# Weight slabs split in two halves and a straight-line GpSimd program in a two-layer retention, Fourier and convolution backbone

## What is computed

```python
for l in range(2):
    sh1, sc1, g1, sh2, sc2, g2 = split(silu(c) @ w_mod[l] + b_mod[l], 6)   # the same for ctx
    p = (rmsnorm(x) * (1 + sc1) + sh1) @ w_in[l]          # q, k, v, gate, fourier, conv columns
    y = concat([retention(q, k, v) * silu(gate),          # both directions, chunks of 128
                real(fft2(p_fourier)),                    # tokens x channels of a group
                p_b * dwconv3(p_c * p_h)])
    x = x + g1 * (y @ w_out[l])
    h = rmsnorm(x) * (1 + sc2) + sh2
    u = dwconv3(h @ w_up[l], w_conv[l]);  val, gate = split(u, 2)
    x = x + g2 * ((val * silu(gate)) @ w_down[l])
return rmsnorm(x, final_norm_g)
```

## Time and profile before

| | |
|---|---|
| time, median of 3 runs | 1671.29 us (1668.88 to 1674.12) |
| the profiled execution | 1678.89 us, its span 1677.0 us |
| mean granted TensorE clock | 0.976 |
| PE busy | 1600.7 us, 95%, 8780 matmuls |
| DVE busy | 955.4 us, 57% |
| POOL busy | 808.8 us, 48%, 636 instructions |
| slab loads | 210 of 512 KB, 3.3 us each from issue to landing |

### The profile page before, as it was taken

The page is one execution under the profiler, slowest core; times in us unless marked ns, Lnnn a source line. Parts: engine busy times, 40 slices in busy tenths (PEclk is TensorE's granted clock), DMA queues, the critical chain, the costliest instruction groups (busy, mean ns, idle before and its releaser), DMA issues.

```text
span 1677.0 us, 24126 instructions
## 1 busy us (share of the span) xinstructions
PE 1600.7 (95%) x8780; PEld 1332.2 (79%) x8780; DVE 955.4 (57%) x1310; ACT 326.3 (19%) x489; POOL 808.8 (48%) x636
## 2 busy tenths in 40 slices
PE   8989999999989999999999999999989999999997
PEld 2878788778777888888888887877767787887876
DVE  2797554378777775874288648454456441341445
ACT  2502111221312200220022214111222220220220
POOL 1244322465334454444444443443464676666663
PEclk9899999989899999999999999999999999999998
DMA  8344111243133343332333222231122222232222
GB/s 348 119 148 150 45 51 39 85 151 113 63 116 115 118 152 113 113 137 69 107 125 113 88 98 79 83 94 51 63 88 76 89 98 88 100 100 95 93 94 94
DMA packets 49635, 174.46 MB, mean 104 GB/s; under 512 B 6448, under 2 KB 6832, under 8 KB 48560
## 3 DMA queue, kind: packets, MB, share of 16 engines
q1 hardware_dynamic: 45504, 167.79, 29.5%
q10 hardware_dynamic: 4080, 5.94, 1.4%
HBM read 167.41 MB, written 2.10 MB: 101 GB/s over the span
## 4 chain that ended last, share of the span: by engine, by line
PE 48%; DVE 18%; issue 14%; POOL 9%; DMA 8%; ACT 2%; DVEq 1%; ACTq 0%; SPq 0%; POOLq 0%
PE pair L1005 40%; DMA raw<-in_slabs 7%; POOL w_lo L384 5%; DVE aux L616 4%; POOL w_hi L382 3%; DVE tg L947 2%; DVE tv L947 2%; PE pair L1054 2%; DVE hid_lo L975 2%; DVE tv L972 1%; PE aux L1213 1%; DVE modv L619 1%; DVE nt L705 1%; ACT tv L586 1%; ACT hid_hi L594 1%
## 5 line engine op out<-in xcount | busy, mean ns | idle before, releaser
L1005 PE MATMUL pair<-h_hi,w_hi 128*128 128x512 f32 x1888 | 573.9, 362 | 23.1 <-POOL w_lo L384 10.9
L1005 PE MATMUL pair<-h_lo,w_hi 128*128 128x512 f32 x1888 | 566.4, 358 | 5.6 <-DVE h_lo L721 3.8
L1005 PE MATMUL pair<-h_hi,w_lo 128*128 128x512 f32 x1888 | 562.8, 356 | 0.0
L384 POOL TENSOR_TENSOR w_lo<-raw,w_hi 128x1024 fp32r<-128x1024 f32 x210 | 536.7, 2556 | 17.5
L380 POOL TENSOR_TENSOR gate<-ones 128x1 f32<-128x1 f32 x210 | 56.4, 269 | 831.3 <-PE pair L1005 736.1
L1005 PEld LDWEIGHTS pair<-h_hi,w_hi 128*128 128x128 f32 x1888 | 312.7, 191 | 81.3 <-issue 18.8
L1005 PEld LDWEIGHTS pair<-h_lo,w_hi 128*128 128x128 f32 x1888 | 311.3, 190 | 64.6 <-DVE h_lo L721 12.3
L1005 PEld LDWEIGHTS pair<-h_hi,w_lo 128*128 128x128 f32 x1888 | 312.4, 191 | 50.6
L616 DVE CUSTOM_DVE_ANT_0 aux<-mod_slot,c_b 128x1024 f32<-128x1024 f32 x160 | 235.0, 1469 | 6.1 <-DMA mod_slot<-in_mods 3.3
L382 POOL TENSOR_SCALAR w_hi<-raw 128x1024 fp32r<-128x1024 f32 x210 | 224.0, 1067 | 0.1
L911 DVE SCALAR_TENSOR_TENSOR x<-pair,modv,x 128x256 f32 (+3 forms) x96 | 60.6, 658 | 187.7 <-PE pair L1005 187.7
(11 more groups left out here) (137 smaller groups left out, 1073.7 us busy)
## 6 DMA issues: line engine op xcount, KB each, us to landing
raw<-in_slabs SPq DMA_DIRECT2D x210, 512.0 KB, 3.3
mod_slot<-in_mods SPq DMA_DIRECT2D x80, 512.0 KB, 3.3
start_slot<-in_start_mods SPq DMA_DIRECT2D x8, 1024.0 KB, 13.5
x<-in_x SPq DMA_DIRECT2D x4, 768.0 KB, 18.1
rot<-kT ACTq DMA_DIRECT2D x32, 64.0 KB, 2.0
rot<-Y ACTq DMA_DIRECT2D x32, 64.0 KB, 2.1
out<-fin SPq DMA_DIRECT2D x8, 256.0 KB, 2.2
c_b<-in_c SPq DMA_DIRECT2D x1, 512.0 KB, 3.9
```

What stands on the lines that cost most here:

```text
L384: nc.gpsimd.tensor_tensor(w_lo[p][:, :], raw[p][:, :], w_hi[p][:, :].bitcast(fp32), ALU.subtract).then_inc(split, 1)
L1005: ins = nc.tensor.matmul(out[:, a:b], wt, xt[:, a:b], start=first and k == 0, stop=last and k == 2)
```

## The change

Each slab is split in two halves of four tiles. The first half of slab s waits for the landing and for a new count, `half_done[p]`, which TensorE raises after tile 3 of slab s - 2; the second half waits for `done` of slab s - 2. (Behind a context table, whose columns all lie in the first half, the first half waits for `done`.) The second half of a down slab with 7 blocks has 384 columns. TensorE begins a slab when its first half is split and waits for the second ahead of tile 4. `split` now counts four per slab; SyncE's waits are scaled and mean the same. The `gate` product is gone, and GpSimd's program is written out for all 210 slabs with constant waits. In the table products the halves t run outside, the blocks b inside, with a wait for the second half between. The output projection's tiles are stored in the order in which they are used.

```diff
+            def split_half(s, half):
+                p, n = s % 2, s // 2
+                a, b = (0, 4 * P) if half == 0 else (4 * P, slab_blocks(s) * P)
+                if half == 0:
+                    pool.wait_ge(loaded[p], 16 * (n + 1))
+                if n and half == 0 and not narrow(s - 2):
+                    pool.wait_ge(half_done[p], n)
+                elif n:
+                    pool.wait_ge(done, s - 1)
+                nc.gpsimd.tensor_scalar(w_hi[p][:, a:b], raw[p][:, a:b], 1.0, 1.0, ALU.mult, ALU.mult).then_inc(split, 1)
+                pool.wait_ge(split, 4 * s + 2 * half + 1)
+                nc.gpsimd.tensor_tensor(w_lo[p][:, a:b], raw[p][:, a:b], w_hi[p][:, a:b].bitcast(fp32),
                                         ALU.subtract).then_inc(split, 1)
+            for s in range(PLAN["end"]):
+                for half in range(2):
+                    split_half(s, half)
...
-                pe.wait_ge(split, 2 * s + 2)
+                pe.wait_ge(split, 4 * s + 2)
...
+                if n == 4:
+                    pe.wait_ge(split, 4 * s + 4)
...
+                if n == 3:
+                    ins.then_inc(half_done[p], 1)
...
-                    for b in range(FB):
-                        for t in range(2):
+                    for t in range(2):
+                        if t and n < NLC:
+                            pe.wait_ge(split, 4 * sl + 4)
+                        for b in range(FB):
...
+                        if t == 0:
+                            ins.then_inc(half_done[p], 1)
...
-        slabs.append(tiles(np.asarray(w_out)[l], KB))
+        slabs.append(tiles(np.asarray(w_out)[l].reshape(KB, P, D)[Y_ORDER].reshape(D, D), KB))
```

More of the change, by code:

```diff
@@ L63, with slab_blocks, narrow @@
 PLAN = stream_plan()
+def slab_blocks(s):
+    for l in range(DEPTH):
+        for g, n in enumerate(GROUPS):
+            if PLAN[l, "down", g] <= s < PLAN[l, "down", g] + KB:
+                return n
+    return KB
+def narrow(s):
+    return PLAN[0, "dft"] + NLC <= s < PLAN[0, "dft"] + NLC + NCC
 def pair_uses(s):
@@ L153, in build_program @@
     ones = new("ones", [P, 1])
-    gate = new("gate", [P, 1])
     root_probe = new("root_probe", [P, 1])
@@ L238, in build_program @@
     done = sem("slab_done")
+    half_done = [sem(f"half_slab_done{i}") for i in range(2)]
     drained = [sem(f"pair_drained{i}") for i in range(2)]
@@ L287, in load_slabs @@
                     for p in range(2):
-                        sp.wait_ge(split, 2 * (first + p - 1) + 4 * i)
+                        sp.wait_ge(split, 4 * (first + p - 1) + 8 * i)
                         load_slab(first + p + 2 * i, p)
@@ L335, in _ @@
                     for p in range(2):
-                        sp.wait_ge(split, 2 * (s + 1 + p) + 4 * i)
+                        sp.wait_ge(split, 4 * (s + 1 + p) + 8 * i)
                         load_slab(s + 2 + p + 2 * i, p)
@@ L372, in _ @@
             pool.wait_ge(fills, 2)
-            def split_slab(p, n, first):
-                pool.wait_ge(loaded[p], 16 * (n + 1))
-                if not first:
-                    pool.wait_ge(done, 2 * n + (p - 1))
-                nc.gpsimd.tensor_tensor(gate[:, 0:1], ones[:, 0:1], ones[:, 0:1], ALU.mult).then_inc(gate_done, 1)
-                pool.wait_ge(gate_done, 1)
-                nc.gpsimd.tensor_scalar(w_hi[p][:, :], raw[p][:, :], 1.0, 1.0, ALU.mult, ALU.mult).then_inc(split, 1)
-                pool.wait_ge(split, 4 * n + (2 * p + 1))
-                nc.gpsimd.tensor_tensor(w_lo[p][:, :], raw[p][:, :], w_hi[p][:, :].bitcast(fp32),
-                                        ALU.subtract).then_inc(split, 1)
-            for p in range(2):
-                split_slab(p, 0, True)
-            with pool.Fori(1, PLAN["end"] // 2) as i:
-                for p in range(2):
-                    split_slab(p, i, False)
+            def split_half(s, half):
[10 more added lines that the diff above has]
+                nc.gpsimd.tensor_tensor(w_lo[p][:, a:b], raw[p][:, a:b], w_hi[p][:, a:b].bitcast(fp32),
+                                        ALU.subtract).then_inc(split, 1)
+            for s in range(PLAN["end"]):
+                for half in range(2):
+                    split_half(s, half)
         @block.scalar
@@ L1008, in begin, with tile @@
             def begin(p, s, uses):
-                pe.wait_ge(split, 2 * s + 2)
+                pe.wait_ge(split, 4 * s + 2)
                 if uses is not None:
                     pe.wait_ge(drained[p], uses)
-            def tile(p, n, order, hi, lo, cols, ready):
+            def tile(p, s, n, order, hi, lo, cols, ready):
                 k = order[n]
+                if n == 4:
+                    pe.wait_ge(split, 4 * s + 4)
                 hi_ready, lo_ready = ready(n) if ready is not None else (None, None)
@@ L1019, in tile @@
                     pe.wait_ge(*hi_ready)
-                t = slice(n * P, n * P + P) if order is not Y_ORDER else slice(k * P, k * P + P)
+                t = slice(n * P, n * P + P)
                 ins = products(pair[p], cols, (w_hi[p][:, t], w_lo[p][:, t]), hi[:, k, :], lo[:, k, :],
                                n == 0, n == len(order) - 1, lo_ready)
+                if n == 3:
+                    ins.then_inc(half_done[p], 1)
                 if n == len(order) - 1:
@@ L1029, in slab @@
                 for n in range(len(order)):
-                    tile(p, n, order, *rest)
+                    tile(p, s, n, order, *rest)
             def in_turns(n, lag):
@@ L1047, in first_pair @@
                         begin(p, first + p, uses)
-                    tile(p, k, order, hi, lo, cols, ready)
+                    tile(p, first + p, k, order, hi, lo, cols, ready)
             def start_mods(k):
@@ L1139, in _ @@
                     for k in range(KB):
-                        tile(j % 2, k, all_k, h_hi, h_lo, cols, None)
+                        tile(j % 2, q, k, all_k, h_hi, h_lo, cols, None)
                         if j % 2 == 0 or k >= NLC + NCC:
@@ L1172, in _ @@
                             begin(j % 2, slab_, pair_uses(slab_ - j % 2))
-                        tile(j % 2, k, all_k, h_hi, h_lo, cols, None)
+                        tile(j % 2, slab_, k, all_k, h_hi, h_lo, cols, None)
                         continue
```

4 lines of the change are left out of this document (2 added, 2 removed).

## The result

The changed kernel takes 1663.93 us (median of 9 runs, 1657.95 to 1669.98); the kernel before took 1672.19 us beside it (9 runs, 1668.88 to 1676.02). The ratio is 0.9946, its 95% interval 0.9932 to 0.9961: faster by 0.5%. The forecast was 1659.5 us in a range of 1648 to 1674. The profiled execution of the changed kernel happens to be its slowest run, 1669.98 us (span 1668.1), so both kernels were profiled a second time; those two executions, 1671.95 and 1663.93 us, lie on the medians, and the accounting further down rests on them.

What follows compares the result with a forecast made beforehand. The prediction took TensorE's 19.7 us of waits for GpSimd, 1.2% of the span, as the prize. Its terms, -1.5 - 7.5 - 2.3 - 6.1 + 1.5 + 4.1, gave -11.8 us: 1671.29 to 1659.5 us, range 1648 to 1674.

Steps and rivals of the forecast that it cites:

- (e): Starts of the four normed phases: first halves now run beside VectorE's h_lo, +1.5 us, between 0 and +3.
- (a): Layer 0 k/v/q slabs: late landings stay, only 1.7 us of waiting can go, once; -1.5 us, between 0 and -2.5.
- (b): Layer 0 token transforms and first output slab: earlier halves -4.5, clock -4.0, VectorE's h_lo +1.0; -7.5 us, between -2 and -9.
- (f): Layer 0 feed-forward: group-end waits +6.9, bad start gone -5.3, clock +2.5; +4.1 us, between -6 and +30.
- (c): Layer 1 token transforms and output: GpSimd's waits go, the h_lo wait takes some back; -2.3 us, between -1 and -2.9.
- (d): Layer 1 feed-forward: waits -6.1, clock -3.2, collisions with VectorE +3.2; -6.1 us, between -1 and -9.
- What bounds the kernel: TensorE's idle time caused by GpSimd, 19.7 us or 1.2% of the span, is the upper end of the direct gain.
- The price of a half: GpSimd's split of 512 columns: 0.62 and 1.30 us, ready 2.0 us after its release instead of 3.7.
- Clean: Rival: collisions between GpSimd and VectorE cost nothing; -22.7 us, 1648.6 us; chance 0.22.
- VectorE becomes the bound: Rival, layer 0 feed-forward: phases never settle, 18.3 us per iteration against 16.64; +8 in all, 1679 us; chance 0.17.
- The wait changes its name: Rival: gains in (a) to (d) are eaten by loads and h_lo, about 1671 us; no change got chance 0.13.
- near -22: Forecast sum without the shared-port rule, so no (e) and no cost in (d) and (f); with the rule, -12.

Runs made afterwards that it cites:

- e4: Changed kernel, with the unread second half of the two context tables split in one column instead of 512: 1658.47 us.
- e6: Changed kernel with both halves released at the end of slab s - 2 and the unread context-table half split in one column: 1646.13 us.
- e7: e6, but in layer 1 a first half is again released in the middle of slab s - 2: 1648.73 us.
- e8: e6, but the first half of the third slab of each layer 1 down group is released early: 1641.90 us.
- e10: e8, with the w_lo of each half made in two instructions of 256 columns: 1642.27 us.
- e1: Kernel before, whole slabs, with GpSimd's program written out with constant waits and without the gate product: 1669.14 us.
- e2: Changed kernel, but both halves wait for the end of slab s - 2; TensorE still begins on a first half: 1650.65 us.
- e3: Changed kernel with its early release, but TensorE begins a slab only when both halves are split: 1670.17 us.
- e5: Changed kernel, but from the third slab on w_lo is made for one column of each half, so the result is wrong: 1629.79 us.
- e9: Changed kernel, but both halves are released at the end of slab s - 2 and TensorE begins only when both are split: 1666.75 us.

## Why the prediction came out, step by step

Ends of slabs, changed minus before, second pair of profiles (first pair in brackets), in us:

| stretch | forecast | measured |
|---|---|---|
| start phase to the first pair's end | part of (e) | +4.5 (+4.6) |
| (a) layer 0 k, v, q | -1.5 | -3.6 (-2.5) |
| layer 0 mixers | 0 | -0.6 (+3.4) |
| (b) layer 0 token transform and output | -7.5 | -1.1 (-1.9) |
| (f) first up group of layer 0, with its start | -5.3 | -3.5 (-8.1) |
| (f) from the first down group to layer 0's last | +9.4 | +9.8 (+9.7) |
| layer 1 k and v start, with its norm | part of (e) | +2.7 (+1.1) |
| layer 1 mixers, with the rest of k, v, q | 0 | -1.8 (-0.2) |
| (c) layer 1 token transform, output | -2.3 | -3.6 (-3.6) |
| (d) layer 1 feed-forward | -6.1 | -11.8 (-11.1) |

(The first norm of layer 0's feed-forward stands in the fifth row, that of layer 1's in the last.) The total is -8.9 by the slabs' ends and -8.0 by the two executions' times; forecast -11.8.

That the total came near is in good part luck. By the second pair, (b), (e) and (f) came out worse than forecast, by 6.4, 5.7 and 2.2 us, and (d), (a), (c) and the mixers better, by 5.7, 2.1, 1.3 and 2.4. (a) to (e) lie outside the ranges that were given for them, and only (f) inside; the errors cancel to 3 us.

**What bounds the kernel** was right: the waits for GpSimd were the prize, and 11 of the 19.6 us went. That nothing else would move by much was not: waits for VectorE and ScalarE rose and fell by several us in half a dozen places. **The price of a half** was right to 0.03 us where VectorE is not in its way.

**(a)** The mechanism was right, the size too small: the longest wait fell from 4.6 to 2.9 us, the 1.7 forecast, and the other two went altogether. In the second pair it fell from 4.4 to 2.6, one of the others went, and the rest of the 3.6 us is the clock, which has a stretch at 0.50 from 108 us in before and none there in the changed kernel. That "the next landing absorbs what the earlier slab won" is the step that was too cautious.

**(b) failed.** The step "two more bring the first output slab's to 343.6" took the halves at 1.9 us each and put VectorE's interference at +1.0 in all. In the rows of the context tables above, `w_hi` took 1.32 and 1.41 us instead of 0.62 and `w_lo` up to 1.85 beside VectorE's `h_lo`, so the two halves took 6.0 us (344.77 to 350.75) and not 3.8. The first of them is the all-zero half of the last context table, which nobody needed. The first output slab began at 350.8 (348.1 before). That isn't to be held against 343.6 as it stands, since the changed kernel was 5.5 us late when the transform began (322.7 against 317.3). Laid from there, the last context slab's first half was ready at 339.3 on the old clock, with 339.8 forecast, and the first output slab at 345.3 with 343.6 forecast: 2.8 us sooner than before instead of 4.5. The wait only moved: 3.2 us at the context transform became 4.3 at the output slab. And the clock, for which 4.0 us were put down, fell there again, for 7 us instead of 10 (3 instead of 7 in the second pair), worth 1.7. Removing the unread half gave back 5.5 us. The earlier first halves held: TensorE lost 1.1 us instead of 3.2 for GpSimd up to that point. Whether the order of the table products had a part in it no run shows apart. A gain that no step had is the shorter wait for `G_lo` (1.6 us, rows above).

**(c)** was right on GpSimd: the 2.9 us of waits for it went, and TensorE waited 1.7 us for VectorE's `h_lo` as before. The deduction for that `h_lo` didn't come true, and `G_lo` gave 1.2 us more (a wait of 1.8 us became 0.6), so 3.6 were measured, beyond the 2.9 of the range.

**(d)** The waits went to the last (6.1 us in four places before; the list of the kernel after has no GpSimd from 1260 us on), and so did the two clock stretches (3.3). The deduction of 3.2 us for collisions inside the iterations was the error: layer 1's up slabs take 10.88 us a pair before and after. VectorE is lengthened there, but nobody waits for it. The rest, some 2 us, is none of the steps: a down slab of eight tiles takes 5.49 instead of 5.60 us from start to start, one of seven 4.81 instead of 4.90, in every kernel with halves and in none with whole slabs; over the 24 down slabs that is 2.4 us. What makes the tile 700 or 687 ns stays open.

**(e)** held in mechanism (1.17 us in the rows at 59 us; `h_lo` 9.3 and 8.0 us of waiting against 3.8 and 5.4), but it was larger than forecast and paid in more places than the four phases: `Y` (3.0 to 4.1) and `ktok` (0.9 to 3.2 and 1.7) of the mixers. At the start of layer 1 the clock is at 0.50 for 10 us in the second profile of the changed kernel and for 7 in that of before, but for 10 in both of the first: that 1.7 us is chance. The some 3.3 us left of the +4.5 in the start phase come from the products of the start vectors at half the clock from 36 us on:

```profile
36.00:42.00 6.00, 6.00 (x9) 0.51 0.35 105
```

against this in the kernel before:

```profile
36.00:42.00 6.00, 5.14 (x30) 1.00 0.39 124
```

Whether that belongs to the change isn't settled. It is in both profiles of the changed kernel and in neither of before, and in those of e4, e6, e7, e8 and e10. It isn't in e1, e2, e3, e5 and e9. So it is not the early release: e6, e8 and e10 release late there and have it, e3 and e5 release early and don't. What sets it stays open.

**(f)** was the step that was feared, and its total was near. At the last block of a group, second profile of the changed kernel (VectorE; then TensorE's wait):

```profile
935.05 0.74 DVE L962 SCALAR_TENSOR_TENSOR tg<-pair,vecs,tg 128x511 f32<-128x511 f32 x1
...
937.64 2.06 DVE L631 CUSTOM_DVE_ANT_0 aux<-mod_slot,c_b 128x1024 f32<-128x1024 f32 x1
...
943.36 0.62 PE L1020 MATMUL pair<-hid_hi,w_hi 128*128 128x512 f32 x2 [2.72 <-ACT hid_hi L609]
```

VectorE is behind, as laid out: the taps of `tg` stand behind two dots, then a dot takes 2.06 instead of 1.22 us. The three waits for `hid_hi` were 1.1, 2.7 and 2.7 us in the second profile, 0.6 before, and two of them have 3.4 us at 0.50 behind them: 5.9 + 3.4 us, where 6.9 + 2.5 were laid out. In the first profile they were 1.1, 1.2 and 2.7 with one such stretch, 4.4 + 1.7, and 2.2 us of the 9.7 are the slower rhythm (last section) of the second up group: there the agreement is luck. The tile waited for was `hid_hi`, one step earlier in the chain than the `hid_lo` forecast. With the release at the end the same taps come ahead of the dots and the wait at this place is 0.2 us. The wait of the first group, 1.1 us, is 1.4 with the late release, and there is none with whole slabs: that one comes from the halves. The bad start went, as forecast; it was smaller than in the profile I had.

**The rivals.** "Clean" was not the change's outcome. Its late-release form comes near the number, 1650.65 us against 1648.6, but not by the same sum: there are collisions in it, and its waits for VectorE and ScalarE are 8 to 10 us shorter than before, which the clean case didn't have. "VectorE becomes the bound" did not occur: layer 0's up pairs, but for the very first, take 16.6 to 17.1 us. "The wait changes its name" describes (b).

**The skill's rule.** The Trainium skill, "SBUF — State Buffer", section "Who interferes with whom", has the second engine blocked until the first one's instruction is over. The trace agrees: with 2.0 us of a `w_lo` left VectorE paid 1.8, with 0.25 left 0.1, and the dots paid likewise. My conclusion from it, that smaller instructions don't reduce the sum, was wrong: they are met more often, but only what is left is paid, and VectorE's busy time fell by 50 us. The "near -22" with the rule left out is the clean rival's sum, too; the forecast's own terms without (e) and the costs in (d) and (f) make -26.

## What to carry to other kernels

When a producer is split finer, two things change, when the consumer may begin and when the producer is let go, and they are to be tried apart: here the first was worth 16 us alone and the second cost 11 to 13. The finer grain itself is a third: it shortened the waits for others by 11 us and lengthened those for the split by 9, until TensorE could begin on a half. Work released earlier than anybody needs it isn't free if it holds up an engine that stands on the path; let it start where that engine is idle, and earlier only in the places where its result is waited for. And before a queue in front of a wait is made finer, look for work in it that nobody reads.

## What the runs showed of the hardware

TensorE has two rhythms in layer 0, at a granted clock of 1.00 and with nothing waited for. The same loop, first in the second profile of the changed kernel, then in its first (rows of two matmuls each, 512 and 256 columns):

```profile
699.64 0.51 PE L1020 MATMUL pair<-h_hi,w_hi 128*128 128x512 f32 x2
...
700.68 0.51 PE L1020 MATMUL pair<-h_hi,w_hi 128*128 128x512 f32 x2
```

```profile
699.70 0.51 PE L1020 MATMUL pair<-h_hi,w_hi 128*128 128x512 f32 x2
...
700.76 0.51 PE L1020 MATMUL pair<-h_hi,w_hi 128*128 128x512 f32 x2
```

1.04 against 1.06 us for six matmuls, 16.64 against 16.96 us for two slabs. A rhythm often holds for a whole group of slabs; the first profile has it slow from 642 to 760 us, the second fast. With some 30 such pairs in the kernel that is up to 10 us of spread between executions of one program, more than the change is worth. Profiles that are compared slab by slab must have it taken out first. What sets it is open.
